# Two modulation blocks placed behind the last retention head, and the first head's decay products, norm and gate placed sooner

## The chip, the cores and the metric

The kernel runs on one core of one Trainium2 chip. The metric is the device time of one execution in microseconds (us). Before the change three runs took 1714.41, 1715.15 and 1715.36 us; their median is 1715.15 us.

The engines are named TensorE (PE in the profile, its weight loads PEld), VectorE (DVE), ScalarE (ACT), GpSimd (POOL) and SyncE (SP, which here only issues DMAs).

## What is computed

A first block and then a second block of two layers, on 256 tokens of width 1024, in float32. The first block, cut to what matters here:

```python
q, k, v, g_ret, x_lru, g_lru = split(rms_norm(x) @ w_in)          # 1024 x 6144
o_ret = group_norm_heads(retention(rotary(q), rotary(k), v))      # 8 heads of 128, decay matrix per head
y_ret = o_ret * silu(g_ret)
xc    = causal_conv(x_lru)                                        # width 4
a     = exp(-8 * sigmoid(xc @ gate_a) * softplus(-lambda))
b     = sqrt(1 - a * a) * sigmoid(xc @ gate_x) * xc
y_lru = scan(h = a * h + b) * silu(g_lru)
x     = rms_norm(x + concat(y_ret, y_lru) @ w_out)
```

The second block works on these 256 tokens ("x") and on 256 context tokens. Each layer first needs a modulation vector for both:

```python
mod   = silu(c)     @ w_mod[l] + b_mod[l]       # 1024 x 6144, six vectors of 1024
mod_c = silu(c_ctx) @ w_mod[l] + b_mod[l]
h     = rms_norm(x) * (1 + scale) + shift       # scale, shift from mod; context: from mod_c
```

Then come mLSTM, grouped-query attention and neighbourhood attention, a gated merge, and a convolutional feed-forward net.

## The kernel before

**Weights.** All large weights come as one stream of 356 pieces of 128 x 1024 elements (512 KB), numbered from 0. Pieces 0 to 47 are w_in (twelve column blocks "in 0" to "in 11" of four pieces each), 48 to 63 the first block's w_out. A piece is loaded by SP into one of four places of w_raw (line 636), copied with rounding by ScalarE into w_hi (line 1185), and VectorE subtracts the two into w_lo (line 1730). TensorE does each product three times (hi x hi, hi x lo, lo x hi, line 695). A piece can be loaded when VectorE has split the one four before it, and copied to w_hi when TensorE has used the one four before it.

**Order.** Each engine's order is written out by hand. On ScalarE split_hi(n) copies all pieces below n, on VectorE split_lo(n) splits all pieces below n, and ahead(key) does as many as TensorE will have used when the bank of that key is full, plus three. The engines wait for each other by semaphores alone.

**The first block's middle.** TensorE puts small steps of the retention between its large products, one step for every four slots (two slots are one weight piece), from "in 5" on: step s does the scores of head s (lines 760 and 761), the output product of head s-1 (lines 768 to 770, which waits for the decay products of that head) and the turn of head s-2 (line 777, which waits for its gate). VectorE's side of it is:
- ret_decay(h), lines 1834 to 1843: it splits ahead for ("rs", h), waits for the scores, and multiplies them by the decay matrix into sT. For head 0 this means all pieces up to 24, for head 1 up to 26, for head 2 up to 28.
- ret_stats and ret_norm, lines 1845 to 1873: mean and variance of both token tiles, variance plus epsilon (line 1862), a wait for ScalarE's square root (line 1271), the reciprocal (line 1865), and the normalised head into onrm (line 1871).
- ret_gate(h), line 1879: times silu(g_ret). ret_lo(h), line 1884: the low part of the turned head.
- lru_scan(n), line 1913: one scan of 256 steps; lru_i times xc, line 1952, is one product over all eight heads, which waits for ScalarE's square root of line 1305.

On ScalarE the same stretch holds, in this order: exponentials (lines 1295 and 1301) with the copies of pieces 22 to 25 between them, the square root over 128 x 2048 elements (line 1305), the copy of piece 26 at the head of tok(5, ...), the silu of "in 5" (line 1265), and ret_sqrt(0) (line 1271).

**Modulation blocks.** The 96 blocks of w_mod (48 for each layer, 128 x 1024 each) are products on VectorE (line 1786): for each block two operations over 1024 elements, one for the context and one for x, with a sum along the row. mod_ops(2) does one block of layer 0. The first 16, which give shift and scale of the first norm, are done in the first block; mod_bias (line 1802), norm_gains (lines 2032 and 2034) and norm_diag (lines 2049 and 2051) follow behind the sixteenth, and TensorE's norm product (line 791) waits for both diagonals. Their loads are SP's too (line 655): the list of mod_after() says behind which piece of the stream a block is loaded; the first 16 have four places, so a block's load waits until the block four before it has been used, and everything behind it on SP waits as well.

```python
after = mod_after()
for p in range(NPIECES):
    if p >= RING: sp.wait_ge(lo_ready, p - RING + 1)
    sp.dma_start(w_raw[:, s, :], wst[p])
    while m < len(after) and after[m] <= p:
        if earlier is not None: sp.wait_ge(mod_used, earlier + 1)
        sp.dma_start(mod_slot[slot], mods_in[m]); m += 1
```

**The end of the first block.** Behind "in 11" TensorE does w_out for the scan's half (pieces 48 to 55), for heads 0 to 3 (56 and 57), then the context's norm (line 791), pieces 58 and 59, and the last four pieces by token tile (line 894). VectorE adds the result to x (line 2104) and the first block's norm follows.

Of the kernel before, what the change touches and what calls it, by code (L numbers as in the profile page):

```python
# [10 lines left out]
ALU = mybir.AluOpType  # L11
# [21 lines left out]
EPS = 1e-6  # L33
# [93 lines left out]
def mod_after():  # L127


    at = [5, 6, 7, 9, 12, 15, 18, 21, 24, 27, 30, 34, 37, 40, 42, 44]  # L130
    at += [FIRST_GA + 7 + 3 * i // 4 for i in range(8)]
    at += [FIRST_MERGE + 4, FIRST_MERGE + 6]
    for first in (4, 12, 18, 24, 30):
        at += [FIRST_MERGE + first + 4 + 2 * i // 3 for i in range(6)]
    for c in range(FB // 2):
        at += [FIRST_UP + 4 * c + 5 + i for i in range(2 if c < 4 else 4)]
    at += [FIRST_DOWN + 4 + i for i in range(4)]
    return at
# [12 lines left out]
def build(nc, wst, mods_in, c_in, x_in, ctx_in, vec_in, tab_in, rot_in, decay_in, gatew_in, rowg_in, gout_in, bias_in, out, plan,  # L151
# [6 lines left out]
    def sb(name, shape, at, dt=F32):  # L158
        return nc.alloc_sbuf_tensor_at(name, shape, dt, offset=base + int(at))
# [68 lines left out]
    at = [C]  # L228

    def small(name, shape, dt=F32):  # L230
        n = 4 * int(np.prod(shape[1:]))
        t = sb(name, shape, at[0], dt)
        at[0] += (n + 31) // 32 * 32
        return t
# [14 lines left out]
    att = small("att", [P, 4, 4])  # L249
# [12 lines left out]
    bnst = sb("bnst", [P, 4, 8], rows_at + 128)  # L262
# [143 lines left out]
    class Counter:  # L406
# [6 lines left out]
        def next(self, key):  # L413
            self.n += 1
            plan[(self.name, key)] = (self.name, self.n)
            return self.sem, 1
# [66 lines left out]
    ret_var = Counter("ret_var")  # L483
# [48 lines left out]
    def psum(key):  # L532
        return bank[plan.get(("bank", key), (0, 1))[0]]

    def filled_at(key):
        kind, b, n, _ = plan.get(("filled", key), ("bank", 0, 1, 0))
        return bank_filled[b] if kind == "bank" else piece_used, n

    def drained_at(key):
        b, n = plan.get(("bank", key), (0, 1))  # L540
        return bank_drained[b], n
# [51 lines left out]
    A, W = Steps("act_chain"), Steps("dve_chain")  # L593

    with nc.Block() as block:

        @block.sync
        def _(sp):
# [26 lines left out]
            for l in range(LAYERS):  # L625
                store_at[piece("w_in_2", l, 9)] = l, "mix"
                load_at[piece("w_out_2", 0, 0) + 4 if l == 0 else piece("w_in_2", l, 13) + 4] = l, "mix"
                store_at[piece("w_up", l, 4)] = l, "ffn"
                load_at[piece("w_down", l, 0) + 5] = l, "ffn"
            after = mod_after()  # L630
            m = 0
            for p in range(NPIECES):
# [1087 lines left out]
        def _(dve):  # L1720
            v = nc.vector
            lo_done = [0]

            def split_lo(upto):

                while lo_done[0] < min(upto, NPIECES):
                    p = lo_done[0]
                    dve.wait_ge(hi_ready, p + 1)
                    used = slice(0, USED_COLS[p])
                    v.tensor_tensor(w_lo[:, p % RING, :, used], w_raw[:, p % RING, :].rearrange("p (k n) -> p k n", k=KP)[:, :, used],  # L1730
                                    w_hi[:, p % RING, :, used].bitcast(F32), ALU.subtract).then_inc(lo_ready, 1)
                    lo_done[0] += 1

            def ahead(key, more=0):
                split_lo(plan.get(("filled", key), (0, 0, 0, 0))[3] + RING - 1 + more)
# [33 lines left out]
            v.tensor_scalar(lam[:, 1, :], lam[:, 2, :], -16.0, None, ALU.mult).then_inc(*W.tell(lam_scaled, 0))  # L1769

            after = mod_after()

            def modulations():
# [19 lines left out]
            def mod_ops(n):  # L1793

                for _ in range(n):
                    next(mods, None)

            def mod_bias(l, j0, j1, sets, done):

                dve.wait_ge(mod_used, done)  # L1800
                b = V(f"b_mod{l}", j0, j1 - j0).unsqueeze(2).to_broadcast([P, j1 - j0, sets])
                v.tensor_tensor(modT[:, l, j0:j1, 0:sets], modT[:, l, j0:j1, 0:sets], b, ALU.add).then_inc(*W.next())
# [31 lines left out]
            def ret_decay(h):  # L1834
                key = ("rs", h)
                ahead(key)
                dve.wait_ge(*filled_at(key))
                ps = psum(key)
                if h >= 2:
                    ahead(("ro", h - 2))  # L1840
                    dve.wait_ge(*filled_at(("ro", h - 2)))
                v.tensor_tensor(sT[:, h % 2, 0:T], ps[:, 0:T], decay[:, h, :], ALU.mult).then_inc(*W.next())
                v.tensor_tensor(sT[:, h % 2, T:T + P], ps[:, T:T + P], decay[:, h, 0:P], ALU.mult).then_inc(*W.drain(key))

            def ret_stats(h):
                key = ("ro", h)
                ahead(key)
                dve.wait_ge(*filled_at(key))
                ps = psum(key)
                for t in range(NT):  # L1850
                    v.bn_stats(bnst[:, t, 0:6], ps[:, t * P:(t + 1) * P]).then_inc(*W.next())
                    dve.wait_ge(*W.last())
                    v.bn_aggr(att[:, 2 * (h % 2) + t, 0:2], bnst[:, t, 0:6]).then_inc(*W.next())
                dve.wait_ge(*W.last())
                return key

            def ret_norm(h):

                key = ret_stats(h)
                ps = psum(key)  # L1860
                mu = att[:, 2 * (h % 2):2 * (h % 2) + 2, 0]
                v.tensor_scalar(bnst[:, 2 + h % 2, 0:2], att[:, 2 * (h % 2):2 * (h % 2) + 2, 1], EPS, None, ALU.add)\
                    .then_inc(*W.tell(ret_var, h))
                dve.wait_ge(*ret_root.at(h))
                v.reciprocal(bnst[:, 2 + h % 2, 2:4], bnst[:, h % 2, 6:8]).then_inc(*W.next())
                dve.wait_ge(*W.last())
                if h >= 2:
                    ahead(("ry", h - 2))
                    dve.wait_ge(*filled_at(("ry", h - 2)))
                for t in range(NT):  # L1870
                    v.tensor_scalar(onrm[:, h % 2, t * P:(t + 1) * P], ps[:, t * P:(t + 1) * P], mu[:, t:t + 1],
                                    bnst[:, 2 + h % 2, 2 + t:3 + t], ALU.subtract, ALU.mult)\
                        .then_inc(*(W.drain(key) if t == NT - 1 else W.next()))
# [7 lines left out]
            def ret_lo(h):  # L1881
                ahead(("ry", h))
                dve.wait_ge(*ret_hi.at(h))
                v.tensor_tensor(mix_lo[:, h, :], psum(("ry", h))[:, 0:T], mix_hi[:, h, :].bitcast(F32), ALU.subtract)\
                    .then_inc(*W.drain(("ry", h)))
# [24 lines left out]
            def lru_scan(n):  # L1910

                dve.wait_ge(*lru_a.at(n))
                v.tensor_tensor_scan(xc[:, n, :], lru_r[:, n, :], lru_i[:, n, :], 0.0, ALU.mult, ALU.add).then_inc(*W.next())
# [28 lines left out]
            dve.wait_ge(*lru_e2.at(HEADS - 1))  # L1942
            v.tensor_scalar(xc[:], xc[:], 1.0, -1.0, ALU.min, ALU.mult).then_inc(*W.tell(lru_clamped, 0))
            split_lo(24)
            mod_ops(2)
            split_lo(25)
            mod_ops(2)
            split_lo(26)
            dve.wait_ge(decay_loaded, 16)
            ret_decay(0)  # L1950
            dve.wait_ge(*lru_mult.at(0))
            v.tensor_tensor(lru_i[:], lru_i[:], xc[:], ALU.mult).then_inc(*W.next())
            dve.wait_ge(*W.last())
            ret_decay(1)
            ret_norm(0)
            for n in range(3):
                lru_scan(n)
            for g in range(2):
                ahead((("in", 5), g))
                dve.wait_ge(*drained_at((("in", 5), g)))  # L1960
            ret_gate(0)
            ret_decay(2)
            lru_scan(3)
            ret_norm(1)
            ret_gate(1)
            ret_lo(0)
            lru_scan(4)
            ret_decay(3)
            lru_scan(5)
            ret_norm(2)  # L1970
            ret_gate(2)
            ret_lo(1)
# [47 lines left out]
            ret_lo(5)  # L2020
            ret_lo(6)
            ret_lo(7)
            mod_ops(2)
            mod_bias(0, 0, 16, 2, 16)
            def norm_gains(l, which):

# [69 lines left out]
            for t in range(NT):  # L2096
                for c in range(2):
                    key = (("out", c), t)
# [73 lines left out]
            for l in range(LAYERS):  # L2172
# [150 lines left out]
                for j in range(4):  # L2323
                    key = ("gqT", l, j)
# [4 lines left out]
                for j in range(2):  # L2329
                    key = ("gkT", l, j)  # L2330
# [66 lines left out]
                key = ("acol", l)  # L2397
# [218 lines left out]
                for c in range(FB // 2 + lag):  # L2616
                    for g in range(4 // per if c < FB // 2 else 0):
                        key = (("up", l, c), g)
# [193 lines left out]
```

## Time and profile before

| | |
|---|---|
| median of the runs | 1715.15 us |
| the profiled execution, its own time | 1714.71 us |
| its span, first to last instruction | 1712.9 us |
| mean granted TensorE clock | 0.998 |
| TensorE busy, matmuls | 1678.2 us, 98% |
| VectorE busy | 1256.1 us, 73% |
| ScalarE busy | 832.2 us, 49% |
| DMA | 254.91 MB, mean 149 GB/s |

The profile is one execution. Busy time of TensorE is modelled and reaches 98% also where matmuls are spread out, so it says little about how much could be saved; the idle times in front of an instruction, in brackets in the timeline, say more. The chain that ended last is followed back from the last instruction, at each step to what released it. Start times are counted from the start of the span. An instruction's duration on VectorE or ScalarE overlaps the next one's start by some 0.08 to 0.1 us, so a sequence is best measured from start to start. The granted clock is a share of TensorE's full 2.4 GHz; 0.50 is 1.2 GHz.

### The profile page before, as it was taken

What the parts mean: (1) busy time and instruction counts of PE and PEld (TensorE: products, weight loads), DVE (VectorE), ACT (ScalarE), POOL (GpSimd) and SP (SyncE); (2) the same over time, 40 slices, a digit from 0 to 9 for tenths busy, and PEclk for the clock granted to TensorE, in tenths of its full rate; (3) what the DMA queues carried; (4) which work ended last, traced back from release to release, by engine and by line L of the source; (5) the groups of instructions that cost most, each with busy time, mean ns of one, the idle gap of its engine ahead of it and who ended that gap; (6) DMA issues with size and microseconds to landing.
All of it is one profiled execution on the core that took longest, in us unless ns stands there. A gap on an engine that the chain in (4) does not pass through costs nothing.

```text
span 1712.9 us, 25308 instructions
## 1 busy us (share of the span) xinstructions
PE 1678.2 (98%) x9872; PEld 1435.6 (84%) x9872; DVE 1256.1 (73%) x2202; ACT 832.2 (49%) x1346; POOL 0.2 (0%) x4
## 2 busy tenths in 40 slices
PE   9989999999999999999999999999999999999998
PEld 9888888777787778889888888888778989979997
DVE  7999767874779798856877776347756786678774
ACT  6665545553334444345444442336453455466653
POOL 0000000000000000000000000000000000000000
PEclk9999999999999999999999999999999999999999
DMA  8646532231235344542455556224322444547653
GB/s 341 225 161 242 188 136 86 87 136 62 63 100 167 121 142 173 208 137 97 138 134 197 197 197 221 97 76 136 99 87 62 128 153 145 169 159 173 196 195 126
DMA packets 79078, 254.91 MB, mean 149 GB/s; under 512 B 14320, under 2 KB 18672, under 8 KB 78320
## 3 DMA queue, kind: packets, MB, share of 16 engines
q1 hardware_dynamic: 73488, 244.91, 43.1%
q10 hardware_dynamic: 5472, 8.39, 1.4%
q8 instruction: 79, 1.29, 0.3%
q14 instruction: 39, 0.32, 0.1%
HBM read 252.19 MB, written 1.07 MB: 148 GB/s over the span
## 4 chain that ended last, share of the span: by engine, by line
PE 78%; DVE 14%; ACT 4%; issue 3%; DMA 0%; ACTq 0%; SPq 0%; DVEq 0%
PE bank L695 65%; DVE w_lo L1730 3%; PE bank L829 3%; PE bank L1000 2%; PE bank L986 2%; PE bank L1078 2%; PE bank L977 2%; DVE mod_w L1786 1%; PE bank L791 1%; ACT w_hi L1185 1%; DVE probT L1786 1%; PE bank L1067 1%; DVE att L2279 1%; DVE xc L1829 1%; DVE bank L2277 0%
## 5 line engine op out<-in xcount | busy, mean ns | idle before, releaser
L1730 DVE TENSOR_TENSOR w_lo<-w_raw,w_hi 128x1024 fp32r<-128x1024 f32 (+1 forms) x356 | 426.7, 1210 | 256.9 <-ACT w_hi L1185 255.5
L1185 ACT ACTIVATE w_hi<-w_raw 128x1024 fp32r<-128x1024 f32 (+1 forms) x356 | 370.1, 1048 | 343.3 <-PE bank L695 287.6
L695 PE MATMUL bank<-hT_hi,w_hi 128*128 128x512 f32 (+1 forms) x1280 | 446.1, 349 | 1.7 <-ACT zo L1455 0.6
L695 PE MATMUL bank<-hT_hi,w_lo 128*128 128x512 f32 (+1 forms) x1280 | 437.7, 342 | 0.0
L695 PE MATMUL bank<-hT_lo,w_hi 128*128 128x512 f32 (+1 forms) x1280 | 437.5, 342 | 0.0
L695 PEld LDWEIGHTS bank<-hT_hi,w_hi 128*128 128x128 f32 x1280 | 242.7, 190 | 30.2 <-issue 2.3
L695 PEld LDWEIGHTS bank<-hT_hi,w_lo 128*128 128x128 f32 x1280 | 242.6, 190 | 28.1
L695 PEld LDWEIGHTS bank<-hT_lo,w_hi 128*128 128x128 f32 x1280 | 242.9, 190 | 26.9 <-issue 1.0
L1786 DVE SCALAR_TENSOR_TENSOR mod_w<-mod_w,c_rows 128x1024 f32<-128x1024 f32 x96 | 117.0, 1218 | 8.4 <-DMA mod_w<-in_mod_weights 8.4
L695 PE MATMUL bank<-w_hi,hT_hi 128*128 128x512 f32 x272 | 114.5, 421 | 0.0
L695 PE MATMUL bank<-w_lo,hT_hi 128*128 128x512 f32 x272 | 106.7, 392 | 0.0
L695 PE MATMUL bank<-w_hi,hT_lo 128*128 128x512 f32 x272 | 106.4, 391 | 0.0
L2632 DVE SCALAR_TENSOR_TENSOR conv<-bank,vec,conv 128x510 f32<-128x510 f32 (+1 forms) x176 | 103.1, 612 | 3.4
L695 PE MATMUL bank<-w_hi,fT_hi 128*128 128x512 f32 x264 | 102.8, 390 | 0.0
L695 PE MATMUL bank<-w_hi,fT_lo 128*128 128x512 f32 x264 | 102.8, 389 | 0.0
L695 PE MATMUL bank<-w_lo,fT_hi 128*128 128x512 f32 x264 | 102.7, 389 | 0.0
L695 PE MATMUL bank<-xT_hi,w_hi 128*128 128x256 f32 x256 | 74.5, 291 | 2.6 <-DVE w_lo L1730 1.6
L695 PE MATMUL bank<-xT_lo,w_hi 128*128 128x256 f32 x256 | 73.1, 285 | 0.0
L695 PE MATMUL bank<-xT_hi,w_lo 128*128 128x256 f32 x256 | 73.0, 285 | 0.0
L1701 ACT ACTIVATE conv<-bank,vec 128x512 f32<-128x512 f32 (+1 forms) x88 | 56.1, 669 | 26.9 <-PE bank L695 26.5
L695 PE MATMUL bank<-yT_hi,w_hi 128*128 128x512 f32 (+1 forms) x192 | 66.6, 347 | 0.0
L695 PE MATMUL bank<-yT_hi,w_lo 128*128 128x512 f32 (+1 forms) x192 | 64.7, 337 | 0.0
(373 smaller groups left out, 2799.8 us busy)
## 6 DMA issues: line engine op xcount, KB each, us to landing
w_raw<-in_weights SPq DMA_DIRECT2D x356, 512.0 KB, 4.1
mod_w<-in_mod_weights SPq DMA_DIRECT2D x96, 512.0 KB, 4.0
nbias<-in_window_bias ACTq DMA_DIRECT2D x32, 128.0 KB, 3.0
resid_c<-in_ctx ACTq DMA_DIRECT2D x2, 1024.0 KB, 5.4
gain_mix<-gain_rows SPq DMA_DIRECT2D x3, 512.0 KB, 5.5
gain_ffn<-gain_rows SPq DMA_DIRECT2D x3, 512.0 KB, 4.0
c_rows<-in_conditions SPq DMA_DIRECT2D x1, 1024.0 KB, 5.8
gatew<-in_gate_weights SPq DMA_DIRECT2D x1, 1024.0 KB, 11.6
```

The source lines that it names most:

```text
L695: mm = pe.matmul(held[key][:, oc], st, mv_, start=(opens and k == 0 and t == 0 and i == 0), stop=(closes and k == tiles - 1 and t == 2), s ...
L791: mm = pe.matmul(ps[:, o:o + P], resid[t // 2][:, t % 2, k * P:(k + 1) * P], diag[:, t, :], start=True, stop=True)
L829: mm = pe.matmul(held[key][:, o], st, mv_, start=opens, stop=(k == KD - 1 and t == 2), skip_group_check=True)
L977: mm = pe.matmul(ps[j][:, 0:n], q_of(kind, q_lo, h + j, cols), k_of(kind, k_lo, h + j, n), start=(i == 0), stop=(i == 2), skip_group_check ...
L986: mm = pe.transpose(ps[:, j * P:(j + 1) * P], prob[:, prob_of(h, t), j * P:(j + 1) * P], ident)
L1000: mm = pe.matmul(ps[i * HD:(i + 1) * HD, h // 2 * P:(h // 2 + 1) * P], v_[:, j, g * HD:(g + 1) * HD], turned_of(kind, h + i)[:, j * P:(j + ...
L1078: mm = pe.matmul(ps[:, j * (P + 1):(j + 1) * (P + 1)], ml_w[:, d, s, t * P:(t + 1) * P], mv[:, s, h, :], start=(s == keys[0]), stop=(s == ...
L1185: a.activation(w_hi[:, p % RING, :, used], w_raw[:, p % RING, :].rearrange("p (k n) -> p k n", k=KP)[:, :, used], ACT.Copy).then_inc(hi_re ...
L1701: a.activation(conv[:, q, conv_cols(c)], psum(key)[:, j * nq:(j + 1) * nq], ACT.Identity, scale=V(f"ffn_w{l}", 2 * FB + blk), bias=V(f"ffn ...
L1730: v.tensor_tensor(w_lo[:, p % RING, :, used], w_raw[:, p % RING, :].rearrange("p (k n) -> p k n", k=KP)[:, :, used], w_hi[:, p % RING, :, ...
L1786: mm = v.scalar_tensor_tensor(product, w, 1.0, c_rows[:, s, :], ALU.mult, ALU.mult, accum_out=modT[:, l, j, s:s + 1])
L2632: v.scalar_tensor_tensor(dst, src, V(f"ffn_w{l}", tap * 2 * FB + blk), dst, ALU.mult, ALU.add)\
```

## The change

Two modulation blocks are no longer done between the splits of pieces 23 and 25; the blocks behind them move up by two places each, and the last call does three blocks in place of one. In mod_after() the loads of blocks 11 to 15 come behind pieces 38, 40, 42, 44 and 46 in place of 34, 37, 40, 42 and 44. The decay products of head 0 stand ahead of the split of piece 25, those of head 1 and the first head's statistics ahead of the product of line 1952; the first head's norm and gate ahead of all scans; and all four first scans behind the decay products of head 2. ret_norm is divided in two functions. No instruction is added or removed.

```diff
 def mod_after():
-    at = [5, 6, 7, 9, 12, 15, 18, 21, 24, 27, 30, 34, 37, 40, 42, 44]
+    at = [5, 6, 7, 9, 12, 15, 18, 21, 24, 27, 30, 38, 40, 42, 44, 46]
...
             def ret_norm(h):
-                key = ret_stats(h)
+                ret_var_of(h)
+                ret_normed(h)
+            def ret_var_of(h):
+                ret_stats(h)
+                v.tensor_scalar(bnst[:, 2 + h % 2, 0:2], att[:, 2 * (h % 2):2 * (h % 2) + 2, 1], EPS, None, ALU.add)\
+                    .then_inc(*W.tell(ret_var, h))
+            def ret_normed(h):
+                key = ("ro", h)
                 ps = psum(key)
                 mu = att[:, 2 * (h % 2):2 * (h % 2) + 2, 0]
-                v.tensor_scalar(bnst[:, 2 + h % 2, 0:2], att[:, 2 * (h % 2):2 * (h % 2) + 2, 1], EPS, None, ALU.add)\
-                    .then_inc(*W.tell(ret_var, h))
                 dve.wait_ge(*ret_root.at(h))
...
             split_lo(24)
-            mod_ops(2)
-            split_lo(25)
-            mod_ops(2)
-            split_lo(26)
             dve.wait_ge(decay_loaded, 16)
             ret_decay(0)
+            split_lo(26)
+            ret_decay(1)
+            ret_var_of(0)
             dve.wait_ge(*lru_mult.at(0))
             v.tensor_tensor(lru_i[:], lru_i[:], xc[:], ALU.mult).then_inc(*W.next())
-            dve.wait_ge(*W.last())
-            ret_decay(1)
-            ret_norm(0)
-            for n in range(3):
-                lru_scan(n)
+            ret_normed(0)
             for g in range(2):
-                ahead((("in", 5), g))
                 dve.wait_ge(*drained_at((("in", 5), g)))
             ret_gate(0)
             ret_decay(2)
-            lru_scan(3)
+            for n in range(4):
+                lru_scan(n)
             ret_norm(1)
             ret_gate(1)
             ret_lo(0)
...
             ret_lo(7)
-            mod_ops(2)
+            mod_ops(6)
             mod_bias(0, 0, 16, 2, 16)
```

## Rows read from the trace of the kernel before

**Rows 1.** The page's chain that ended last, shares of the span by engine:

```profile
PE 78%; DVE 14%; ACT 4%; issue 3%; DMA 0%; ACTq 0%; SPq 0%; DVEq 0%
```

**Rows 2.** TensorE's waits, 80 to 260 us: total us, times, longest:

```profile
PE bank L768 <- issue: 3.6, 1, 3.6
PE bank L791 <- DVE diag L2051: 2.2, 1, 2.2
...
PE bank L695 <- DVE w_lo L1730: 1.3, 3, 0.5
```

**Rows 3.** Timeline of VectorE, 85 to 105 us: start, duration, line, operation:

```profile
85.50 1.22 DVE L1786 SCALAR_TENSOR_TENSOR probT<-mod_w,c_rows 128x1024 f32<-128x1024 f32 x1
...
92.35 0.41 DVE L1842 TENSOR_TENSOR sT<-bank,decay 128x256 f32<-128x256 f32 x1
...
92.95 2.29 DVE L1952 TENSOR_TENSOR lru_i<-lru_i,xc 128x2048 f32<-128x2048 f32 x1
95.28 1.23 DVE L1730 TENSOR_TENSOR w_lo<-w_raw,w_hi 128x1024 fp32r<-128x1024 f32 x1
...
99.18 1.84 DVE L1913 TENSOR_TENSOR_SCAN xc<-lru_r,lru_i 128x256 f32<-128x256 f32 x3
101.16 0.43 DVE L1879 TENSOR_TENSOR onrm<-onrm,sg 128x256 f32<-128x256 f32 x1
...
104.91 0.27 DVE L1851 BATCH_NORM_STATS2 bnst<-bank 128x6 f32<-128x128 f32 x1
```

**Rows 4.** Windows of ScalarE: stretch, length, busy, granted clock, DMA share, GB/s:

```profile
84.40:93.00 8.60, 8.57 (x14) 1.00 0.52 183
```

**Rows 5.** Timeline of ScalarE, 86 to 94 us:

```profile
86.10 1.05 ACT L1185 ACTIVATE w_hi<-w_raw 128x1024 fp32r<-128x1024 f32 x1
...
89.72 1.28 ACT L1305 ACT_TABLE_LOAD   x1
91.01 1.91 ACT L1305 ACTIVATE xc<-xc 128x2048 f32<-128x2048 f32 x1
92.83 1.04 ACT L1185 ACTIVATE w_hi<-w_raw 128x1024 fp32r<-128x1024 f32 x1
```

**Rows 6.** Windows of TensorE, the granted clock in the fourth column:

```profile
94.00:95.00 1.00, 1.00 (x7) 0.50 0.62 258
...
124.00:125.00 1.00, 0.85 (x7) 1.00 0.23 90
...
237.00:238.00 1.00, 1.00 (x6) 0.50 0.07 16
```

**Rows 7.** Timeline of TensorE: head 3's turn, context norm, piece 63:

```profile
124.15 0.44 PE L777 MATMUL bank<-tab,onrm 128*128 128x128 f32 x2 [1.66 <-DVE onrm L1879]
...
206.91 3.73 PE L791 MATMUL bank<-diag,resid_c 128*128 128x128 f32 x32
...
220.56 0.47 PE L894 MATMUL bank<-w_hi,mix_hi 128*128 128x512 f32 x1 [0.38 <-issue]
```

**Rows 8.** Timeline of VectorE: block 11's second operation, and the splits of 46 and 47:

```profile
159.91 1.22 DVE L1786 SCALAR_TENSOR_TENSOR mod_w<-mod_w,c_rows 128x1024 f32<-128x1024 f32 x1
...
166.15 2.35 DVE L1730 TENSOR_TENSOR w_lo<-w_raw,w_hi 128x1024 fp32r<-128x1024 f32 x2
```

**Rows 9.** SP's issue of piece 47; us to landing of pieces 42 and 38:

```profile
158.88 0.33 SPq L636 DMA_DIRECT2D w_raw<-in_weights  x1
...
w_raw<-in_weights SPq DMA_DIRECT2D x1, 512.0 KB, 5.0
...
w_raw<-in_weights SPq DMA_DIRECT2D x1, 512.0 KB, 6.2
```

**Rows 10.** Timeline of VectorE: first diagonal, splits of 58 and 59, split of 63:

```profile
204.19 0.17 DVE L2049 RECIPROCAL ss<-rs 128x1 f32<-128x1 f32 x1 [1.18 <-ACT rs L1343]
...
205.96 2.35 DVE L1730 TENSOR_TENSOR w_lo<-w_raw,w_hi 128x1024 fp32r<-128x1024 f32 x2
...
219.24 1.22 DVE L1730 TENSOR_TENSOR w_lo<-w_raw,w_hi 128x1024 fp32r<-128x1024 f32 x1
```

## Prediction, made before the changed kernel had run

> **What bounds the kernel now.** I read the chain that ended last first [rows 1]: most of the span is TensorE's, so time can be won or lost only where TensorE waits. The view of its waits from 80 to 260 us [rows 2] shows where that is in the first block: 3.6 us at line 768, the product of head 0 that needs VectorE's first decay product; 2.2 us at line 791, the second half of the context's and the latent's norm; and three short waits, 1.3 us in all, for w_lo of a weight piece. The rest of the span behind 260 us does the same instructions in the same order with or without the change, and TensorE bounds it; so I look for one number, the shift of TensorE's work where it leaves the first block.
>
> Around the 3.6 us I read both helpers. VectorE [rows 3] runs the four operations of blocks 7 and 8 from 85.50 us and gets to the decay product at 92.35 us, with nothing but work before it. That reads as a VectorE that is the bound. But ScalarE is just as full there: busy 8.57 of 8.60 us [rows 4]. Its order [rows 5] is a w_hi copy at 86.10 (piece 24), exponentials, the copy of piece 25, a table load, the long square root, and only at 92.83 us the w_hi copy of piece 26. VectorE's split of piece 26 (95.28 us in rows 3) needs that copy.
>
> **Term 1, the middle: +0.5 us.** Two blocks leave: four operations of 1.14 us from start to start (85.50, and the next split or operation 1.14 later), 4.6 us of VectorE. What VectorE can do with them:
> - Decay product 0 is led by the split of piece 24, whose w_hi is there at 86.10 + 1.05 = 87.15 us. Split 1.14, two products 0.6: sT is ready at 88.9 us, not 93.0. TensorE asked at 93.07 - 3.60 = 89.5 us, so the stall at line 768 goes. The half clock behind it goes too: the granted clock was 0.50, the 1.2 GHz level, in 94 to 95 us [rows 6].
> - Decay product 1 is led by the split of piece 26 (line 1836, filled after piece 24, plus RING - 1). Its w_hi ends at 92.83 + 1.04 = 93.87 us whatever VectorE does, since ScalarE's chain waits for nothing of VectorE that is late. VectorE idles about 3 us and starts this split at 93.91 instead of 95.28: 1.37 us of the 4.6 are left.
> - From this split to the second head's norm it was 104.91 - 95.28 = 9.63 us. Now the long product of line 1952 (92.95 to 95.28, 2.33 us) lies in that stretch, as it stands behind the first head's statistics; against it go the 0.27 us wait for the root, which that product covers, and about 0.17 us between the scans and the gate (three scans of 0.6 took from 99.18 to 101.16). So 93.91 + 9.63 + 2.33 - 0.45 = 105.42 us: 0.5 us **later** than before.
> - Gate 0 itself is ready sooner: 101.16 - 95.28 = 5.88 from the split, plus 2.33, less the 1.98 of scans now behind it and 0.27: start 93.91 + 5.96 = 99.87, end 100.3 us, before 101.6. TensorE, free of its stall, gets to the turn of head 0 at about 97.1 us (two weight pieces and two small steps after 89.5) and stalls there for about 3.2 us. What the stall at line 768 gave is waited off here.
> - Whatever TensorE still has ahead ends at head 3's turn: it waited 1.66 us for VectorE's gate there already [rows 7], VectorE's order from head 1 on is unchanged, and so this turn comes 0.5 us later. Bounds of the term: -3.2 us (VectorE never waits for ScalarE: -4.58 - 0.27 - 0.1 and + 1.77 for the scans that now stand before head 1's norm), +0.5 (the rows as they stand). I take +0.5, since the ScalarE rows fix it.
>
> Here one page bears on the size. The table load at 89.72 took 1.28 us and the next activation started 0.01 us after it [rows 5]. The Trainium skill, page "ScalarE: Activation LUTs", section "What ACT_TABLE_LOAD costs", adds a drain of about 1.38 us to each load. By it w_hi of piece 26 would be 1.4 us later and the sum 1.4 us larger; the trace disagrees, and the row is taken.
>
> **Term 2, the queues: +0.4 us.** From 125 us on VectorE does as much as before between the same splits (blocks 7 and 8 stand where 9 and 10 stood), and it bounds TensorE, which waits for w_lo three times [rows 2]; so the 0.5 us stay. SP is another matter: a block's load (line 655) waits until the block four before it has been used, and SP holds the weight pieces behind it. Blocks 11 to 15 now wait for blocks 7 to 11, which VectorE does late. Piece 39 waits for block 7 and piece 43 for block 9, each some 3 to 6 us; their w_lo splits stand behind the rotations, about 3 us behind their new landing, and I cost them at nothing (without that cover: up to 3 us each). Piece 47 is closest. It was issued at 158.88 us [rows 9]; now block 15's load stands before it and waits for block 11's second operation, 159.91 + 1.22 + 0.5 = 161.7 us [rows 8], plus 0.43 for its own issue: 162.15. The landing nearest to this case, a piece with one block's load issued 0.4 us from it, took 5.0 us; one with more in flight took 6.2 [rows 9]. With 5.0 and 1.05 for w_hi it is ready at 168.2, and VectorE wants it at 166.15 + 1.14 + 0.5 = 167.8 us: 0.4 us late. Bounds 0 (landing below 4.6) and 1.6 (6.2). The statistics of head 4, ScalarE's root, silu and gate 4 hang on it without slack, so it passes on.
>
> **Term 3, the end: +2.5 us.** Behind ret_lo(7) six operations stand instead of two: 4 x 1.145 = 4.58 us in front of the bias, the gains and the two diagonals that TensorE's norm (line 791) waits for. Cover: VectorE waited 1.18 us for ScalarE's root there, and again before the second diagonal; without waits the two reciprocals and diagonals take 4 x 0.2 us from 203.01, so they would end at 203.81 and not 205.96 [rows 10]. Cover 2.15, left 2.4 to 2.5 us. TensorE was at line 791 at 206.91, just 0.9 us behind the diagonals [rows 7]: it now waits some 1.6 us. VectorE's order behind that (splits of 58 and 59, four context norms with splits between, the split of piece 63 at 219.24) is serial with ScalarE, and TensorE waited for this last split at 220.56 already; so the whole 2.47 us arrive there, and the chain product, add, square, root, scaling starts from it. Nothing of the 4.58 is removed from the kernel. Bounds: 0 (if line 894 had the slack, which its wait excludes) and 4.6.
>
> **Sum:** 0.5 + 0.4 + 2.5 = +3.4 us on the profiled execution's 1714.71 us (span 1712.9 and 1.8 around it), 1718.1. The median of the runs lies 0.44 above that execution: **1718.5 us**. A measurement of this kernel tells about 0.2%, 3.4 us, from no change: the bounds are 1711.7 and 1718.6.
>
> **Rivals.**
> - *VectorE's work alone decides the middle.* The Trainium skill, page "Perfetto Trace Analysis", section "Optimization Strategies", tells to relieve the engines that block the critical path when the matmul engine waits for them; the case is this rule taken at its word. If piece 26 didn't hold decay product 1, term 1 would be -3.2, and -3.2 + 2.5 = -0.7 us, 1714.4. For: VectorE's row has no gap before 92.35. Against: ScalarE's 8.57 of 8.60 us. 0.15. For a result below 1711.7 the last blocks would have to be hidden as well: 0.04.
> - *Half clock behind the new wait at line 791 (slower).* The 1.66 us wait left the granted clock at 1.00, a 2.2 us wait at this same line was followed by 0.50 [rows 2, 6, 7]. If the new 1.6 us wait counts as the second, TensorE loses about 1.9 us in the transposes and products, of which its 1.3 us wait for piece 63 covers all but 0.7: +4.1 us, 1719.2. It decides from a wait between 1.7 and 2.2 us on. 0.12.
> - *Piece 47 lands after 6.2 us.* Term 2 becomes 1.6: +4.6 us, 1719.7. It decides above 4.6 us. For: block 15's load and piece 48 are in flight with it. 0.08.
> - *The change does not do what it says*: the plan of banks is TensorE's and stays; no line adds an operation. Nothing speaks for it.
>
> **How the numbers follow.** The forecast has 0.6, and its own spread (1717.3 to 1719.3) lies on both sides of 1718.6, so it gives 0.3 to each. Within 0.2%: 0.3 + 0.15 + 0.03 = 0.48. Slower: 0.3 + 0.12 + 0.08 - 0.02 for overlap = 0.48. Faster 0.04. The range goes from the first rival (1714.4) to a late piece 47 together with half clock, 1720.8.
>
> **What would show it.** In the changed profile: no wait at line 768, whose product starts near 89.4; an idle VectorE from about 90.9 to 93.9, released by w_hi; a new TensorE wait of about 3 us at line 777 near 97 to 100; statistics of head 1 at 105.4; head 3's turn at 124.7; w_lo of piece 47 at 168; last mod_w near 206.5; line 791 starting at 209 to 209.5 after a wait of 1.6; line 894's wait for piece 63 grown to 1.3. The forecast is wrong if w_hi of piece 26 comes before 92 us, if head 3's turn starts before 124.1, or if line 791 follows line 695 without a wait.

## The result and the profile after

The changed kernel takes 1717.38 us (median of 19 runs, 1716.71 to 1718.81), the one before 1714.62 us (19 runs, 1713.64 to 1715.57): 2.76 us slower, a ratio of 1.0017 with a 95% interval of 1.0010 to 1.0023. The forecast was +3.4 us on the profiled execution (1718.5 us against runs of 1715.15), the range 1714.4 to 1720.8. 0.17% is below the 0.2% that counted as a change in the forecast. A ratio of 1 lies outside the interval and 1.002 inside it: the kernel did get slower, by 0.10% to 0.23%.

In the two profiles the same work of the first block starts some tenths of a us apart, already before anything that the change touches. This offset differs from execution to execution (from -0.02 to 0.96 us against the kernel before, in the runs below), and its cause was not looked into. So I measure every start from the split of piece 23, the last operation of VectorE that both kernels do in the same place. VectorE executes 2202 operations before and after; only one of its waits fell away with the new order. Before, from VectorE's timeline:

```profile
84.36 1.22 DVE L1730 TENSOR_TENSOR w_lo<-w_raw,w_hi 128x1024 fp32r<-128x1024 f32 x1
```

After, the same view (line 1960 is the product of line 1952 before, 1888 the gate, 1851 the statistics; columns as in [rows 3], in brackets the idle time ahead and its releaser):

```profile
84.96 1.22 DVE L1730 TENSOR_TENSOR w_lo<-w_raw,w_hi 128x1024 fp32r<-128x1024 f32 x1
87.85 1.23 DVE L1730 TENSOR_TENSOR w_lo<-w_raw,w_hi 128x1024 fp32r<-128x1024 f32 x1 [1.68 <-ACT w_hi L1185]
...
90.33 1.22 DVE L1730 TENSOR_TENSOR w_lo<-w_raw,w_hi 128x1024 fp32r<-128x1024 f32 x1 [0.71 <-ACT w_hi L1185]
94.50 1.22 DVE L1730 TENSOR_TENSOR w_lo<-w_raw,w_hi 128x1024 fp32r<-128x1024 f32 x1 [2.95 <-ACT w_hi L1185]
...
97.19 2.28 DVE L1960 TENSOR_TENSOR lru_i<-lru_i,xc 128x2048 f32<-128x2048 f32 x1
...
100.45 0.43 DVE L1888 TENSOR_TENSOR onrm<-onrm,sg 128x256 f32<-128x256 f32 x1
...
105.94 0.27 DVE L1851 BATCH_NORM_STATS2 bnst<-bank 128x6 f32<-128x128 f32 x1
```

Look at the three idle times: 1.68 + 0.71 + 2.95 = 5.3 us, all released by ScalarE's copies, where VectorE had none before. Two things left the stretch ahead of the split of piece 26: the two blocks (4.6 us) and the long product (2.3 us), which now stands behind that split. Of these 6.9 us the idle times took 5.3; the split starts only 1.4 us sooner (9.54 us behind the split of piece 23 and not 10.92). Head 0's gate starts 15.49 us behind the split of piece 23 and not 16.80 [rows 3]; the statistics of head 1, behind all four scans now, 20.98 and not 20.55 us. ScalarE's own timeline has not moved (after):

```profile
86.70 1.05 ACT L1185 ACTIVATE w_hi<-w_raw 128x1024 fp32r<-128x1024 f32 x1
...
90.31 1.28 ACT L1305 ACT_TABLE_LOAD   x1
...
93.42 1.04 ACT L1185 ACTIVATE w_hi<-w_raw 128x1024 fp32r<-128x1024 f32 x1
```

Against [rows 5] these are 0.60, 0.59 and 0.59 us later, which is the common offset of 0.60. TensorE after the change:

```profile
89.89 0.39 PE L768 MATMUL bank<-v,sT 128*128 128x128 f32 x2
...
100.93 0.44 PE L777 MATMUL bank<-tab,onrm 128*128 128x128 f32 x2 [3.12 <-DVE onrm L1888]
...
125.20 0.64 PE L777 MATMUL bank<-tab,onrm 128*128 128x128 f32 x2 [2.64 <-DVE onrm L1888]
...
209.91 3.81 PE L791 MATMUL bank<-diag,resid_c 128*128 128x128 f32 x32 [1.81 <-DVE diag L2055]
...
224.33 0.47 PE L894 MATMUL bank<-w_hi,mix_hi 128*128 128x512 f32 x1 [1.06 <-issue]
```

The 3.6 us wait at line 768 [rows 2] is gone; a 3.12 us wait for head 0's gate has taken its place, head 3's turn waits 2.64 us and not 1.66 [rows 7], line 791 has a new wait, and the one for piece 63 has grown from 0.38 to 1.06. At the end, VectorE's timeline after, from the first operation of blocks 13, 14 and 15 on:

```profile
200.73 1.22 DVE L1786 SCALAR_TENSOR_TENSOR probT<-mod_w,c_rows 128x1024 f32<-128x1024 f32 x1
...
203.21 1.23 DVE L1786 SCALAR_TENSOR_TENSOR probT<-mod_w,c_rows 128x1024 f32<-128x1024 f32 x1
...
205.69 1.23 DVE L1786 SCALAR_TENSOR_TENSOR probT<-mod_w,c_rows 128x1024 f32<-128x1024 f32 x1
...
208.94 0.15 DVE L2053 RECIPROCAL ss<-rs 128x1 f32<-128x1 f32 x1
...
209.72 2.35 DVE L1730 TENSOR_TENSOR w_lo<-w_raw,w_hi 128x1024 fp32r<-128x1024 f32 x2
...
223.01 1.22 DVE L1730 TENSOR_TENSOR w_lo<-w_raw,w_hi 128x1024 fp32r<-128x1024 f32 x1
```

The reciprocals no longer wait for ScalarE's roots (before: 1.18 us at the first one in [rows 10], and 0.88 at the second, in the line of before below); that was the cover, and it is used up. The splits of 58 and 59 start at 209.72 against 205.96.

```profile
205.56 0.16 DVE L2049 RECIPROCAL ss<-rs 128x1 f32<-128x1 f32 x1 [0.88 <-ACT rs L1343]
```

### The profile page after: what moved, and what is told of

Same layout as the page of the kernel before. It is cut to its first block, busy times and chain, and to the rows that moved or that the text cites. A ratio compares the mean times of both kernels' runs of the same rounds, so it can differ in the third digit from the quotient of the medians.

```text
span 1717.0 us, 25307 instructions
## 1 busy us (share of the span) xinstructions
PE 1681.1 (98%) x9872; PEld 1438.4 (84%) x9872; DVE 1256.5 (73%) x2202; ACT 832.3 (48%) x1346; POOL 0.2 (0%) x4
## 3 DMA queue, kind: packets, MB, share of 16 engines
HBM read 252.19 MB, written 1.07 MB: 148 GB/s over the span
## 4 chain that ended last, share of the span: by engine, by line
PE 79%; DVE 13%; ACT 5%; issue 3%; DMA 0%; ACTq 0%; SPq 0%; DVEq 0%
PE bank L695 65%; DVE w_lo L1730 3%; PE bank L829 3%; PE bank L1000 2%; PE bank L986 2%; PE bank L1078 2%; PE bank L977 2%; PE bank L791 1%; DVE mod_w L1786 1%; ACT w_hi L1185 1%; DVE probT L1786 1%; PE bank L1067 1%; DVE xc L1829 1%; DVE att L2283 1%; DMA w_raw<-in_weights 0%
```

## The experiments

Theory 1 is the one of the forecast: in the middle VectorE is held by ScalarE's copies, so nothing is won there, and the end bears what VectorE's waits don't cover. The rivals stand with each run. All eight were timed in five rounds beside the kernel before (33 runs: 1714.64 us in the first four, 1714.62 us in the last four). One median of 11 runs has an interval of about 0.09%, 1.5 us, so the place where a start moved is read from the traces. The table gives, in us (+ is later or slower), the shift against the kernel before of three starts, each less the run's own offset at the split of piece 23, and the difference of the medians. For the changed kernel, head 3's turn: 125.20 - 124.15 - 0.60 = +0.45.

| kernel | offset | head 3's turn | piece 63 on TensorE | second norm, line 791 | medians |
|---|---|---|---|---|---|
| changed | 0.60 | +0.45 | +3.17 | +3.17 | +2.76 |
| e1 one block in the gap | 0.89 | +0.44 | +0.61 | +0.61 | +0.87 |
| e2 the end alone | 0.06 | -0.01 | +3.66 | +3.63 | +3.29 |
| e3 the middle alone | 0.14 | +0.43 | +0.37 | +0.35 | +0.58 |
| e4 copy sooner | -0.02 | -0.53 | +2.10 | +2.09 | +1.17 |
| e5 root sooner too | 0.80 | -2.22 | +0.51 | +0.49 | +0.97 |
| e6 and one block in the gap | 0.90 | -2.22 | -2.04 | -2.05 | -1.37 |
| e7 loads later | 0.96 | +0.45 | +3.18 | +3.17 | +3.37 |
| e8 both blocks in gaps | 0.32 | +0.46 | +0.40 | +0.39 | +0.75 |

**e1, one block back into the idle time.** Against the changed kernel:

```diff
             split_lo(26)
+            mod_ops(2)
             ret_decay(1)
...
-            mod_ops(6)
+            mod_ops(4)
```

> One of the two blocks goes back into the middle, between the split of piece 25 and the decay products of head 1, where VectorE idles 2.95 us in the changed kernel; the end has two blocks instead of three. Theory 1 (VectorE waits there for ScalarE's copy of piece 26, the end bears the cost): the 2.3 us of the block fit the idle time, so head 1's statistics and head 3's turn start as in the changed kernel within 0.1 us (measured from the decay product of head 0), and line 791 comes 2.4 us sooner; the kernel is 2.4 us faster than the changed one and 0.5 to 0.9 us slower than the one before. Rival (VectorE's own work bounds the middle, the block's time counts wherever it stands): head 1's statistics come 2.3 us later and the total stays within 0.3 us of the changed kernel.

1715.51 us, +0.87 against before, ratio 1.0005 (0.9996 to 1.0014). VectorE's timeline:

```profile
91.77 1.22 DVE L1786 SCALAR_TENSOR_TENSOR probT<-mod_w,c_rows 128x1024 f32<-128x1024 f32 x1
...
94.80 1.23 DVE L1730 TENSOR_TENSOR w_lo<-w_raw,w_hi 128x1024 fp32r<-128x1024 f32 x1 [0.67 <-ACT w_hi L1185]
...
106.24 0.27 DVE L1851 BATCH_NORM_STATS2 bnst<-bank 128x6 f32<-128x128 f32 x1
```

The block's 2.3 us came out of the idle time (2.95 to 0.67) and moved nothing: 106.24 - 85.25 = 20.99 us from the split of piece 23, 20.98 in the changed kernel. The rival falls. Line 791 came 2.0 us sooner, not 2.4, since it no longer waited at all; piece 63 came 2.56 us sooner. By the medians the kernel is 1.9 us faster than the changed one, where 2.4 was expected.

**e2, the end alone.** Against the kernel before; the sum of the spare operations goes to an unused column:

```diff
+            for _ in range(4):
+                v.scalar_tensor_tensor(probT[:].rearrange("p a t -> p (a t)"), c_rows[:, 0, :], 1.0, c_rows[:, 1, :],
+                                       ALU.mult, ALU.mult, accum_out=ss[:, 63:64]).then_inc(*W.next())
+                dve.wait_ge(*W.last())
             mod_ops(2)
             mod_bias(0, 0, 16, 2, 16)
```

> The kernel before, with four spare operations of the modulation's shape (over data that is there, the sum into an unused column) ahead of the last block: only the end of the change. Theory 1: cover at the end is 2.15 us of the 4.6 to 4.8, so the split of piece 63 and all behind it come 2.5 to 2.7 us later and the kernel is 2.5 to 2.7 us slower than before. Rival (the end has more slack than the waits show, and the loss is in the middle): 0 to 1 us.

1717.93 us, +3.29, ratio 1.0018 (1.0010 to 1.0027). The end alone costs as much as the whole change and somewhat more than expected. TensorE's timeline, its window of 210 to 212 us, and one line of VectorE's timeline:

```profile
209.01 5.43 PE L791 MATMUL bank<-diag,resid_c 128*128 128x128 f32 x32 [1.91 <-DVE diag L2055]
224.28 0.47 PE L894 MATMUL bank<-w_hi,mix_hi 128*128 128x512 f32 x1 [0.27 <-issue]
```

```profile
210.00:212.00 2.00, 2.00 (x12) 0.50 0.36 86
```

```profile
218.93 0.69 DVE L2076 TENSOR_TENSOR hT_lo<-ptmp,hT_hi 128x512 fp32r<-128x512 f32 x1 [1.56 <-ACT hT_hi L1356]
```

The wait at line 791 was 1.91 us, and the 32 transposing products behind it took 5.43 us at a granted clock of 0.50, the 1.2 GHz level, against 3.81 in the changed kernel, where the wait was 1.81 and the window reads 1.00:

```profile
210.00:212.00 2.00, 2.00 (x19) 1.00 0.11 16
```

This is the rival "half clock behind the new wait", seen in e2 and not in the changed kernel's profile. Piece 63 came 3.66 us late here and 3.17 - 0.45 = 2.72 us in the changed kernel for its end part, 0.94 us apart. Two places hold them: the splits of 58 and 59 start 208.82 - 205.96 - 0.06 = 2.80 us late (0.1 more than in the changed kernel; the spare operations each wait for the one before, 1.26 us from start to start), and VectorE then waits 1.56 us for the norm's first result in the line above, where the changed kernel waits 0.70. So the half clock took 1.6 us more on TensorE and passed on 0.86, where the forecast had priced it at 0.7.

**e3, the middle alone.** The changed kernel with blocks 14 and 15 cut to 8 columns of 1024, so their sums are left out of the modulation:

```diff
+                        if m in (14, 15):
+                            product, w = product[:, 0:8], w[:, 0:8]
-                        mm = v.scalar_tensor_tensor(product, w, 1.0, c_rows[:, s, :], ALU.mult, ALU.mult,
+                        mm = v.scalar_tensor_tensor(product, w, 1.0, c_rows[:, s, 0:w.shape[1]], ALU.mult, ALU.mult,
```

> The changed kernel with the products of blocks 14 and 15 cut to 8 of their 1024 columns: their sums are left out of the modulation, everything else stands. Only the middle of the change is left, and the end is that of before or a little shorter than it. Theory 1: the middle alone gives no gain: head 1's statistics 0.4 to 0.5 us later than before (from the start of the clamp's split of piece 23), and the kernel is 0.2 to 0.8 us slower than the one before. Rival (the middle gains and the end takes it away): 2 to 5 us faster than before.

1715.22 us, +0.58, ratio 1.0004 (0.9995 to 1.0013). Statistics of head 1 at 105.48 - 84.50 = 20.98 us, 0.43 later than before; line 791 (the context's norm) without a wait. The middle gains nothing, even with 4.6 us taken out of the kernel; the rival's 2 to 5 us are outside the interval.

**e4, the copy of piece 26 sooner.** On ScalarE, against the changed kernel:

```diff
+            split_hi(27)
             act.wait_ge(*lru_clamped.at(0))
             a.activation(xc[:], xc[:], ACT.Sqrt, bias=1.0).then_inc(*A.tell(lru_mult, 0))
```

> The changed kernel, with ScalarE's copy of piece 26 ahead of its square root instead of behind it. Theory 1 (this copy holds head 1's decay product): VectorE's idle of 2.95 us ahead of the split of piece 26 falls below 0.3; the long product then waits for the square root until about 1.1 us later than that ended before, the gate of head 0 is ready 0.8 to 1.3 us sooner, head 1's statistics come 0.8 to 1.3 us sooner than in the changed kernel, and the kernel is about 1 us faster than the changed one. Rival (VectorE's idle is covered and something else, the root or the silu, holds gate 0): no part of the stretch behind gate 0 moves by more than 0.2 us.

1715.81 us, +1.17, ratio 1.0009 (1.0000 to 1.0018). VectorE's timeline (its lines stand one higher from 1305 on):

```profile
89.71 2.36 DVE L1731 TENSOR_TENSOR w_lo<-w_raw,w_hi 128x1024 fp32r<-128x1024 f32 x2 [0.72 <-ACT w_hi L1185]
...
97.80 0.17 DVE L1875 RECIPROCAL bnst<-bnst 128x2 f32<-128x2 f32 x1 [1.62 <-ACT bnst L1271]
...
104.35 0.27 DVE L1852 BATCH_NORM_STATS2 bnst<-bank 128x6 f32<-128x128 f32 x1
```

The splits of 25 and 26 now run as one pair, the 2.95 us are gone, and head 1's statistics come 0.97 us sooner (20.01 for 20.98); piece 63 comes 1.07 us sooner, and the medians are 1.6 us apart, about 1 expected. So that copy was what held VectorE. The next hold shows at once: 1.62 us for head 0's root, which ScalarE does behind the silu and two table loads.

**e5, the root sooner too.** On ScalarE, against e4:

```diff
+            ret_sqrt(0)
             tok(5, sg, ACT.Silu)
-            ret_sqrt(0)
             ret_sqrt(1)
```

> The kernel of the sooner copy, with ScalarE's root for head 0 behind its long square root and ahead of the silu, not behind it. Theory 1 (from the decay product of head 1 on, ScalarE's order holds VectorE): the reciprocal follows the long product without the 1.3 to 1.5 us of idle, gate 0 is ready 1.2 to 1.4 us sooner than with the sooner copy alone, head 1's statistics too, and the kernel is 1.2 to 1.5 us faster than that one, about as fast as the one before or 0.3 us faster. Rival (TensorE's wait at line 777 moves to head 3 and what is won in front is lost behind it): the starts of head 1's statistics move, line 791 does not.

1715.59 us, +0.97, ratio 1.0006 (0.9997 to 1.0014). Statistics of head 1 1.70 us sooner than in e4 (18.31), head 3's turn 1.69, piece 63 1.59: this exceeds the 1.2 to 1.4 expected, because the wait was 1.62. The medians show only 0.2 us, so the 1.2 to 1.5 us expected of the whole kernel were not seen there. One thing that can hide them is what follows the second wait at line 791, ahead of the second norm. This wait is 2.2 us in every kernel here, before and after. In eight of the ten profiles it was followed by the half clock (before: 5.44 us for the 32 products, 0.50 in [rows 6]); in e4's and e7's not:

```profile
238.38 3.81 PE L791 MATMUL bank<-diag,resid_x 128*128 128x128 f32 x32 [2.19 <-DVE diag L2056]
```

That is 1.6 us between executions of nearly the same program. Whether e4's runs fell on the good side oftener than e5's, and so whether this accounts for the missing us, is not shown: a profile shows one execution.

**e6, one block in the idle time ahead of decay product 0.** Against e5:

```diff
             split_lo(24)
+            mod_ops(2)
             dve.wait_ge(decay_loaded, 16)
             ret_decay(0)
...
-            mod_ops(6)
+            mod_ops(4)
```

> The same, and one block back into the middle, where VectorE idles 1.7 us ahead of the split of piece 24 and 0.7 us ahead of that of piece 25; two blocks stay at the end instead of three. Theory 1: the block takes 2.3 of these 2.4 us, line 768 waits 0.2 to 0.6 us, the end costs 0.2 us instead of 2.7; 2.2 to 2.5 us faster than the run with the root sooner, 1.5 to 2 us faster than the kernel before. Rival (the late decay product 0 costs again what it cost before, with a half clock): within 0.5 us of the kernel before.

1713.25 us, 1.37 us **faster** than before, ratio 0.9988 (0.9979 to 0.9997), a little less than the 1.5 to 2 expected; 2.3 us faster than e5, as expected. Its eleven runs lie in two groups, five from 1711.25 to 1711.64 and five from 1713.25 to 1713.96 (the last is 1717.03), so this median could easily be 1.6 us lower; by the trace piece 63 comes 2.04 us sooner than before. VectorE, then TensorE:

```profile
86.40 1.22 DVE L1787 SCALAR_TENSOR_TENSOR probT<-mod_w,c_rows 128x1024 f32<-128x1024 f32 x1
...
90.63 2.36 DVE L1731 TENSOR_TENSOR w_lo<-w_raw,w_hi 128x1024 fp32r<-128x1024 f32 x2 [0.20 <-ACT w_hi L1185]
...
103.57 0.27 DVE L1852 BATCH_NORM_STATS2 bnst<-bank 128x6 f32<-128x128 f32 x1
```

```profile
90.54 0.46 PE L768 MATMUL bank<-v,sT 128*128 128x128 f32 x2 [0.18 <-issue]
```

The block took the idle times of 1.68 and 0.71 but for 0.20, line 768 waited 0.18 us, and head 1's statistics stand where e5 has them (103.57 - 85.26 = 18.31). The end cost 2.22 - 2.04 = 0.18 us.

**e7, SP's waits.** The changed kernel with the blocks' loads one piece later each:

```diff
-    at = [5, 6, 7, 9, 12, 15, 18, 21, 24, 27, 30, 38, 40, 42, 44, 46]
+    at = [5, 6, 7, 9, 12, 15, 18, 21, 24, 27, 30, 39, 41, 43, 45, 47]
```

> The changed kernel with the loads of blocks 11 to 15 behind pieces 39, 41, 43, 45 and 47, one piece later each, so that SP's waits for used blocks hold other pieces (40, 44, 48) than 39, 43 and 47. Theory 1 (these waits are covered): within 0.3 us of the changed kernel, its split of piece 47 without a wait for a copy. Rival (SP's waits cost part of the loss): 0.4 us or more faster than the changed kernel.

1717.99 us, +3.37, ratio 1.0018 (1.0009 to 1.0027). The medians put it 0.6 us above the changed kernel, more than the 0.3 expected, but well within the 1.5 us interval of such a median, and not on the rival's side. Head 3's turn and piece 63 are where the changed kernel has them to 0.01 us, so other pieces held on SP change nothing, and these waits cost nothing. In the changed kernel itself SP waited five times for a used block, 24.5 us in all and up to 7.2 at once, and still head 4's turn is late by no more than head 3's, 180.40 - 179.35 - 0.60 = +0.45. ScalarE did wait for piece 47, VectorE did not (SP's issue of pieces 47 to 49, then ScalarE, then VectorE, whose second split of this pair is piece 47 and starts at 168.33):

```profile
162.60 2.22 SPq L636 DMA_DIRECT2D w_raw<-in_weights  x3
```

```profile
167.09 1.06 ACT L1185 ACTIVATE w_hi<-w_raw 128x1024 fp32r<-128x1024 f32 x1 [3.43 <-DMA w_raw<-in_weights]
```

```profile
167.19 2.35 DVE L1730 TENSOR_TENSOR w_lo<-w_raw,w_hi 128x1024 fp32r<-128x1024 f32 x2
```

**e8, both blocks in the gaps.** The changed kernel with mod_ops(2) behind split_lo(24) and behind split_lo(26), and mod_ops(2) at the end as before: only the new order is left.

> The changed kernel with both blocks back in the middle, one ahead of the decay product of head 0, one ahead of that of head 1, and one block at the end as before: only the new order of the middle is left, with all its work in it. Theory 1: the two blocks (4.6 us) fit VectorE's idle times of 1.7, 0.7 and 2.95 us, so head 1's statistics and head 3's turn stay where the changed kernel has them, line 791 does not wait, and the kernel is 0.3 to 0.6 us slower than the one before. Rival (only the blocks' leaving made the middle what it is): head 1's statistics 2 us or more later than in the changed kernel.

1715.37 us, +0.75, ratio 1.0003 (0.9994 to 1.0012), somewhat above the 0.3 to 0.6 expected; by the trace +0.40 at piece 63. Head 1's statistics at 105.67 - 84.68 = 20.99 us: with all of its work back, the middle ends where it ended without it. The 4.6 us of work had been worth nothing there, and the 0.4 us are the price of the new order. No run takes the blocks out and keeps the old order. The rows of before say that this would gain nothing either: the long product started at 92.95 [rows 3], and its input was ready only at 91.01 + 1.91 = 92.92 [rows 5]; but that is argued, not measured.

## Why the prediction was right, point by point

- **Term 1, the middle, +0.5 us: right, +0.43 to +0.45 measured.** Each step held: sT sooner, no wait at line 768, VectorE idle ahead of piece 26 (2.95, predicted about 3), head 1's statistics 105.4 predicted and 105.94 - 0.60 = 105.34 found, a wait of 3.12 at head 0's turn (predicted 3.2). e3 shows the term alone, e4 that the copy of piece 26 was its cause, e1 and e8 that the removed work had no price there. The table load stayed 1.28 us, and the next activation started 0.02 us behind it (90.31, then 91.61). The Trainium skill, page "ScalarE: Activation LUTs", section "What ACT_TABLE_LOAD costs", adds a drain to each switch; it does not show here.
- **Term 2, the queues, +0.4 us: mis-sized, it is 0.** Block 15's load and piece 47 went as foreseen (ScalarE waited 3.43 us for it), but the copy ended at 168.15, and VectorE wanted it at 168.33. Less the offset the copy was ready at 167.55, not at 168.2. The term of the sum that was off is the landing: SP issued the load at 162.60, less the offset 0.15 us sooner than foreseen, and the copy began 4.49 us later, not after the 5.0 us that I took from another pair of transfers. The lower bound, 0, was right, by 0.18 us only; e7 shows that other held pieces cost nothing either.
- **Term 3, the end, +2.5 us: right in kind, 0.2 short.** 209.72 - 205.96 - 0.60 - 0.45 = 2.71 us; e4, e5 and e7, with the same end, have 2.63 to 2.73 (piece 63 less head 3's turn). The blocks at the end take 2.48 us each (200.73, 203.21, 205.69) and not 2.29: each waits for the one before to have been used, about 0.19 us that I had not counted between blocks that stand back to back. So two blocks more are 4.96 us and not 4.58, and the cover was 2.25 and not 2.15: without waits the first reciprocal starts 0.09 us behind the gains, not 0.17. TensorE's wait at line 791 was 1.81, predicted 1.6.
- **Sum:** 0.45 + 0 + 2.72 = +3.17 us at piece 63, and the same at the second norm; 3.4 was forecast. It is luck that these are so close: term 2 was 0.4 too high and term 3 0.2 too low. The medians show 2.76. The profiled execution of the changed kernel was the slowest of its 19 (1718.81 us), 4.10 above the profiled one before: 3.17, the offset of 0.60 and 0.33 behind the second norm. The 0.4 between 3.17 and the medians is within what single executions differ by (the half clock alone is 1.6 us) and stays open. The upper end of the range has a slip: 4.6 and 0.7 us on 1715.15 give 1720.45, not 1720.8; nothing hangs on it.
- **Rivals.** "VectorE's work alone decides the middle", the advice of the Trainium skill (page "Perfetto Trace Analysis", section "Optimization Strategies") taken at its word, fell: the engine TensorE waited for was itself held by a third one, ScalarE, as soon as it was relieved. The half clock at line 791 did not come in the changed profile, behind 1.81 us, but did in e2, behind 1.91; the forecast had put the deciding wait between 1.7 and 2.2 us. That piece 47 lands late did not happen.

## What to carry to other kernels

An engine that shows no idle time ahead of a late product is not yet the bound: look at when its inputs are there. Here ScalarE was as full as VectorE, and of the 6.9 us of work taken from in front of the split of piece 26 (two blocks and the long product) 5.3 became waiting; the order on ScalarE (a copy ahead of a long square root, a root ahead of two table loads) gave what the lighter VectorE could not, and then one of the two removed blocks fitted into the idle time that was left. Work that moves to the end of a stage costs all that the waits there don't cover, and only the waits count as cover: 2.25 us of 4.96 here.

## What the runs showed of the hardware that was not expected

- The fall to 1.2 GHz behind a wait is not the same from execution to execution. Behind the 2.2 us wait at the second norm the 32 products took 5.4 us in eight profiles and 3.81 us in two. Behind a wait at the context's norm they took 3.81 us after 1.79 to 1.81 us (changed kernel, e4, e5, e7) and 5.43 us after 1.91 us (e2).
- In the changed kernel the clock also fell behind the 3.12 us and the 2.64 us wait at line 777 (its two windows of TensorE below). In e7, behind the same 3.12 us wait, it stayed at 1.00 (third line, e7's window). It cost nothing: head 3's turn comes +0.45 us in both, because TensorE waits there for VectorE anyway, 3.27 us in e7 (last line) in place of 2.64.

```profile
102.00:104.00 2.00, 2.00 (x11) 0.50 0.40 63
126.00:128.00 2.00, 2.00 (x12) 0.50 0.00 0
```

```profile
102.00:104.00 2.00, 2.00 (x19) 1.00 0.22 33
```

```profile
125.56 0.44 PE L777 MATMUL bank<-tab,onrm 128*128 128x128 f32 x2 [3.27 <-DVE onrm L1888]
```
